# Expert weights laid out by partition, loaded in three transfers of 4 MB instead of eight of 1 or 2 MB

## The reference

```python
def moe_ffn(h, w_router, b_router, w_exp_in, b_exp_in, w_exp_out, b_exp_out):
    logits = (t @ w_router + b_router).astype(jnp.float32)
    top_val, top_idx = lax.top_k(logits, TOP_K)          # 4 of 32
    gate_w = jax.nn.softmax(top_val, axis=-1)
    ...
        hb = xb @ w_exp_in[e] + b_exp_in[e]               # 1024 x 2048
        g = jnp.minimum(hb[:, :D_FF_2], SWIGLU_LIMIT)
        u = jnp.clip(hb[:, D_FF_2:], -SWIGLU_LIMIT, SWIGLU_LIMIT)
        a = g * jax.nn.sigmoid(SWIGLU_ALPHA * g) * (u + 1.0)
        return a @ w_exp_out[e] + b_exp_out[e]            # 1024 x 1024
    ...
    y = jnp.einsum('nk,nkd->nd', gate_w, y_slot)
```

## Time and profile before

| | |
|---|---|
| median of 3 runs | 1470.51 us |
| lowest, highest | 1470.10, 1471.36 |
| span of the profiled execution, first to last instruction | 1468.7 us |
| median less that span | 1.8 us |
| mean granted PE clock | 0.984 |
| PE busy | 1308.1 us, 89% |
| DVE, ACT, POOL busy | 32%, 27%, 15% |
| HBM read | 492.76 MB, mean 336 GB/s over the span |

### The profile page before, as it was taken

One profiled execution on the slowest core, in us unless ns is written; L12 is line 12 of the kernel. 1 busy time (PEld: TensorE's weight loads), 2 busy tenths in 40 slices (PEclk: granted clock), 3 DMA queues, 4 the chain that ended last, 5 costly groups with the idle time before them and its releaser, 6 DMA issues.

```text
span 1468.7 us, 25925 instructions
## 1 busy us (share of the span) xinstructions
PE 1308.1 (89%) x9475; PEld 815.8 (56%) x9476; DVE 469.8 (32%) x916; ACT 390.4 (27%) x728; POOL 222.4 (15%) x129
## 2 busy tenths in 40 slices
PE   7998999999999997887989888988889988997886
PEld 7786999878999853343334433443333434343333
DVE  2756777654534961111102110211011101110112
ACT  5566666555667420010001000110010001000101
POOL 5772112006775300000000000000000000000000
PEclk9999999999999999898999999999999999999998
DMA  9532667855443789999999999999999999999996
GB/s 332 179 101 58 172 184 227 303 193 172 172 173 116 256 333 423 424 428 424 427 424 428 427 427 424 426 428 425 425 428 427 422 424 428 426 427 425 427 427 273
DMA packets 114537, 494.40 MB, mean 337 GB/s; under 512 B 7633, under 2 KB 57153, under 8 KB 81505
## 3 DMA queue, kind: packets, MB, share of 16 engines
q1 hardware_dynamic: 113011, 491.50, 83.3%
q10 hardware_dynamic: 1486, 2.34, 0.5%
HBM read 492.76 MB, written 1.06 MB: 336 GB/s over the span
## 4 chain that ended last, share of the span: by engine, by line
PE 59%; DMA 29%; DVE 5%; issue 4%; ACT 3%; SPq 0%; POOL 0%; DVEq 0%; ACTq 0%
DMA big_mem<-in_w_exp_in 24%; PE ps L1055 16%; PE ps L1097 8%; PE ps L579 6%; PE ps L581 5%; PE ps L580 5%; DMA big_mem<-in_w_exp_out 5%; PE ps L1038 3%; PE ps L797 1%; PE ps L799 1%; PE ps L798 1%; PE ps L1120 1%; PE ps L1111 1%; PE ps L1085 1%; PE ps L599 1%
## 5 line engine op out<-in xcount | busy, mean ns | idle before, releaser
L1055 PE MATMUL ps<-big_mem,ring_mem 128*32 128x512 f32 (+1 forms) x2304 | 366.8, 614 | 53.7 <-DMA big_mem<-in_w_exp_in 53.7
L1055 PEld LDWEIGHTS ps<-big_mem,ring_mem 128*32 128x32 f32 (+1 forms) x2304 | 111.0, 121 | 287.2 <-issue 194.4
L1097 PE MATMUL ps<-big_mem,x 128*32 128x256 f32 (+1 forms) x1888 | 185.1, 436 | 5.3 <-ACT x L1716 3.3
L579 PE MATMUL ps<-hT_hi,w_hi 128*128 128x256 f32 x600 | 171.3, 285 | 1.3 <-DVE hT_lo L1806 1.3
L580 PE MATMUL ps<-hT_lo,w_hi 128*128 128x256 f32 x600 | 169.7, 283 | 0.0
L581 PE MATMUL ps<-hT_hi,w_lo 128*128 128x256 f32 x600 | 169.7, 283 | 0.0
L1038 PEld LDWEIGHTS ps<-ring_mem,h 128*128 128x128 f32 x1024 | 131.6, 197 | 60.1 <-issue 60.1
L1038 PE MATMUL ps<-ring_mem,h 128*128 128x96 f32 x1024 | 148.9, 289 | 0.0
L2312 DVE TENSOR_SCALAR ring_mem<-ps 128x256 f32<-128x256 f32 (+1 forms) x36 | 18.7, 520 | 404.1 <-PE ps L1055 404.1
L1700 ACT ACTIVATE ring_mem<-ring_mem 128x256 f32<-128x256 f32 (+1 forms) x36 | 17.7, 493 | 466.4 <-DVE ring_mem L2312 466.4
L1097 PEld LDWEIGHTS ps<-big_mem,x 128*32 128x32 f32 (+1 forms) x1888 | 71.7, 117 | 104.9 <-issue 67.7
(11 more groups left out here) (430 smaller groups left out, 1736.6 us busy)
## 6 DMA issues: line engine op xcount, KB each, us to landing
big_mem<-in_w_exp_in SPq DMA_DIRECT2D x128, 2048.0 KB, 22.3
big_mem<-in_w_exp_out SPq DMA_DIRECT2D x128, 1024.0 KB, 21.4
ring_mem<-in_w_in SPq DMA_DIRECT2D x14, 2048.0 KB, 8.0
ring_mem<-in_w_up SPq DMA_DIRECT2D x44, 512.0 KB, 4.6
ring_mem<-in_w_down SPq DMA_DIRECT2D x5, 2048.0 KB, 11.1
ring_mem<-in_w_out SPq DMA_DIRECT2D x4, 2048.0 KB, 8.1
ring_mem<-in_w_branch_a SPq DMA_DIRECT2D x1, 2048.0 KB, 7.4
ring_mem<-in_w_branch_b SPq DMA_DIRECT2D x1, 2048.0 KB, 7.7
```

Of the source, the lines that this page charges most:

```text
L579: mm(out, hi, x_hi, start=start, stop=False)
L1055: last = mm(out, stationary, weights[:, f, w * q:w * (q + 1)] if m > XS else weights[:, :, w * q:w * (q + 1)], start=start, stop=stop)
L1097: last = mm(ps[m * q:m * (q + 1), 4 + at // XS, 0:w], aT[:, k % n, k // n, :], wout[:, k, w * q:w * (q + 1)], start=(k == 0), stop=(k == K ...
```

## The change

On the host the two weight arrays are laid out anew: matrix row 128k + p is row k of partition p, and a partition's eight rows lie end to end (64 KB of in-weights, 32 KB of out-weights). The in-weights come in two transfers of four rows k, 4 MB each with 32 KB to a partition; the out-weights in one of eight rows, 4 MB, 32 KB to a partition. PE waits for landings at k = 0 and 4 of the first product and at k = 0 of the second. SP waits for four finished rows ahead of a half of the in-weights and for all eight ahead of the out-weights. As row k now holds the matrix rows 128k to 128k + 127, the gather and the transposes of `a` read 128 columns in order instead of every second one of 256. The amount of data and the number of matmuls stay as they are.

```diff
+WIN_ROWS, WOUT_ROWS = 4, 8
...
-        win_x = ins["w_exp_in_2"].rearrange("l e (k p j) n -> (l e) k p j n", p=P, j=2)
-        wout_x = ins["w_exp_out_2"].rearrange("l e (k p j) n -> (l e) k p j n", p=P, j=2)
+        win_x = ins["w_exp_in_2"].rearrange("e p (h j) n -> e h p j n", j=WIN_ROWS)
+        wout_x = ins["w_exp_out_2"].rearrange("e p (h j) n -> e h p j n", j=WOUT_ROWS)
...
-                for k in range(KD // 2):
-                    sp.wait_ge(s["gu_part"], KD * others + 2 + 2 * k)
-                    sp.dma_start(win[:, 2 * k:2 * k + 2, :], win_x[cur, k]).then_inc(win_in[k], 16)
-                for k in range(KD // 2):
-                    sp.wait_ge(s["y_part"], KD * others + 2 + 2 * k)
-                    sp.dma_start(wout[:, 2 * k:2 * k + 2, :], wout_x[cur, k]).then_inc(wout_in[k], 16)
+                for n in range(KD // WIN_ROWS):
+                    sp.wait_ge(s["gu_part"], KD * others + WIN_ROWS * (n + 1))
+                    sp.dma_start(win[:, WIN_ROWS * n:WIN_ROWS * (n + 1), :], win_x[cur, n]).then_inc(win_in[n], 16)
+                for n in range(KD // WOUT_ROWS):
+                    sp.wait_ge(s["y_part"], KD * others + WOUT_ROWS * (n + 1))
+                    sp.dma_start(wout[:, WOUT_ROWS * n:WOUT_ROWS * (n + 1), :], wout_x[cur, n]).then_inc(wout_in[n], 16)
...
-                        last = mm(ps[:, bank, c:c + SLOTS], h1[:, t, SEQ * (k // 2) + k % 2:SEQ * (k // 2 + 1):2], moe["picks"][:, t, :], start=(t == 0), stop=(t == T - 1))
+                        last = mm(ps[:, bank, c:c + SLOTS], h1[:, t, P * k:P * (k + 1)], moe["picks"][:, t, :], start=(t == 0), stop=(t == T - 1))
...
-                    if k % 2 == 0:
-                        pe.wait_ge(win_in[k // 2], landed_all)
+                    if k % WIN_ROWS == 0:
+                        pe.wait_ge(win_in[k // WIN_ROWS], landed_all)
...
-                    last = nc.tensor.transpose(place, moe["a"][:, KD * at + SEQ * (c // 2) + c % 2:KD * at + SEQ * (c // 2 + 1):2], ident)
+                    last = nc.tensor.transpose(place, moe["a"][:, KD * at + P * c:KD * at + P * (c + 1)], ident)
...
-                    if k % 2 == 0:
-                        pe.wait_ge(wout_in[k // 2], landed_all)
+                    if k % WOUT_ROWS == 0:
+                        pe.wait_ge(wout_in[k // WOUT_ROWS], landed_all)
...
+    for n in ("w_exp_in_2", "w_exp_out_2"):
+        a = np.asarray(inputs[n])[0]
+        given[n] = np.ascontiguousarray(a.reshape(E, KD, P, a.shape[-1]).transpose(0, 2, 1, 3))
```

More of the change, by code:

```diff
@@ L129, in program @@
         s = {n: ctx.enter_context(nc.semaphore(n)) for n in EVENTS}
-        win_in = [ctx.enter_context(nc.semaphore(f"win{k}_in")) for k in range(KD // 2)]
-        wout_in = [ctx.enter_context(nc.semaphore(f"wout{k}_in")) for k in range(KD // 2)]
+        win_in = [ctx.enter_context(nc.semaphore(f"win{h}_in")) for h in range(KD // WIN_ROWS)]
+        wout_in = [ctx.enter_context(nc.semaphore(f"wout{h}_in")) for h in range(KD // WOUT_ROWS)]
         ring_mem = ctx.enter_context(nc.sbuf_tensor("ring_mem", [P, 3 * 4096], F32))
@@ L458, in _ @@
             sp.wait_ge(s["merged_ready"], KD)
-            for k in range(KD // 2):
-                sp.dma_start(win[:, 2 * k:2 * k + 2, :], win_x[0, k]).then_inc(win_in[k], 16)
+            for n in range(KD // WIN_ROWS):
+                sp.dma_start(win[:, WIN_ROWS * n:WIN_ROWS * (n + 1), :], win_x[0, n]).then_inc(win_in[n], 16)
             sp.wait_ge(s["out_ps"], T)
-            for k in range(KD // 2):
-                sp.dma_start(wout[:, 2 * k:2 * k + 2, :], wout_x[0, k]).then_inc(wout_in[k], 16)
+            for n in range(KD // WOUT_ROWS):
+                sp.dma_start(wout[:, WOUT_ROWS * n:WOUT_ROWS * (n + 1), :], wout_x[0, n]).then_inc(wout_in[n], 16)
             sp.wait_ge(s["counts_ready"], 1)
@@ L1134, in _ @@
                     c = SLOTS * (k % EARLY)
-                    last = mm(ps[:, 7 if k < EARLY else 6, c:c + SLOTS], h1[:, t, SEQ * (k // 2) + k % 2:SEQ * (k // 2 + 1):2], moe["picks"][:, t, :],
+                    last = mm(ps[:, 7 if k < EARLY else 6, c:c + SLOTS], h1[:, t, P * k:P * (k + 1)], moe["picks"][:, t, :],
                               start=(t == 0 and k in (0, EARLY)), stop=(t == T - 1), skip_group_check=True)
```

## The result

The changed kernel takes 1487.66 us (median of 4 runs), the kernel before 1470.7 on the same chip: ratio 1.0112, 95% interval 1.01 to 1.0124. It is slower, as forecast, but by 17 us where 6.3 were forecast, and 0.7 us outside the range. The profiled execution is the slowest of the four, 1489.61 with a span of 1487.8, 19.1 above the span before.

What follows compares the result with a forecast made beforehand. The weight stream through the DMA engines was taken to bound the kernel, PE a close second. Terms -9.3 + 3.5 + 9.6 + 1.1 + 1.4 = +6.3 us gave 1476.8 us, 0.4% slower; range 1465 to 1487.

Steps and rivals of the forecast that it cites:

- Pace: Weight stream: a 4 MB transfer takes 9.74 us, a turn 29.22 instead of 29.52, saving 9.3 us over 31 turns.
- Start: First load for turn 1 waits for four rows of the first product instead of two: 3.5 us more.
- Coarser release: Out-weights wait for all eight rows; the stream stands still 2.4 us in each of four 96-token turns: 9.6 us more.
- clock term: Low granted clock lengthens the first product in 96-token turns: 1.1 us more, bounds 0 and 5.4.
- first condition: PE must finish both products of a turn within four transfers, 38.96 us, from its first in-half's landing; 96 tokens need 41.35.
- In-order reads: Gather and transposes load faster on PE: 0.3 us off each 96-token turn, counted within the stall; bounds 0 to 6 us.
- End: Last second product starts all eight rows only after the whole out-weights land: 1.4 us more.
- A: Rival, faster: the stream gains more than PE's stalls give back, 4 MB in 9.60 us: 1466 us, chance 0.17.
- B: Rival, no difference: the gather gains 1 us more per 96-token turn or a transfer takes 9.68: 1472 us, chance 0.2.
- D: Rival, slower: in-weight rows 64 KB apart in memory cost 3% of their load time: 1488 us, chance 0.05.
- C: Rival, slower by more: long rows gain nothing and low clock falls into each 96-token turn: 1486 us, chance 0.15.

Runs made afterwards that it cites:

- e9: Changed kernel's transfer sizes and releases on the old weight layout (rows of 16 KB and 8 KB, strided gather and transposes): 1497.22 us, ratio 1.0181 to the kernel before.
- e1: Changed kernel with its new layout and in-order reads, but transfers of two rows as before: 1471.12 us, ratio 0.9998 to the kernel before.
- e5: Changed kernel with tokens beyond 64 of an expert left out, so 96-slot turns become 64-slot turns: 1468.04 us, ratio 0.997 to the uncapped kernel before.
- e10: Changed kernel with two more matmuls, results unused, behind the first product of each 96-slot turn: 1498.73 us, ratio 1.0179 to the kernel before.
- e11: Kernel before the change with two more matmuls, results unused, in each 96-slot turn: 1473.0 us, ratio 1.0008 to the kernel before.
- e4: Changed kernel with out-weights in two transfers of 2 MB, in-weights still in two of 4 MB: 1483.03 us, ratio 1.0081 to the kernel before.
- e2: Changed kernel with out-weights in four transfers of 1 MB, in-weights still in two of 4 MB: 1487.39 us, ratio 1.0112 to the kernel before.
- e3: Changed kernel with in-weights in four transfers of 2 MB, out-weights still in one of 4 MB: 1489.37 us, ratio 1.0118 to the kernel before.
- e8: Changed kernel with in-weights in four transfers of 2 MB and out-weights in two of 2 MB: 1468.84 us, ratio 0.9976 to the kernel before.
- e12: Changed kernel with four extra matmuls in each 32-slot turn ahead of the wait for the second in-half: 1491.2 us, ratio 1.0146 to the kernel before.
- e7: Changed kernel with ten extra matmuls in each 32-slot turn ahead of the wait for the second in-half: 1566.37 us, ratio 1.0644 to the kernel before.

## Why the prediction was right in its sign and wrong in its size

- **Pace**: right in kind, a little small. 9.3 us were forecast, 11.5 measured; a 4 MB transfer takes 9.71 and not 9.74. That the cost goes by row and not by transfer is shown by e9.
- **Start**: 3.5 forecast, 3.7 measured.
- **Coarser release**: the mechanism is the one forecast, and e1, e5, e10 and e11 show it from four sides. The size is what failed, **the term 4 x 2.4 = 9.6 with its clock term of 1.1: 10.7 us, where the stream lost 24.2, 22.5 of them around the four 96-slot turns.** Turn by turn, from landing of the first half (in the first and fourth worked out from the landing ahead, as PE did not wait there) to data flowing again, less four transfers of 9.71: 4.6, 5.3, 4.1 and 3.6 us, 17.6 in all. Of the 6.9 beyond the forecast, 5.2 are clock: the four first products took 23.47, 24.78, 23.49 and 23.04, 6.3 over 22.1, where I had counted 1.1. 0.6 is the first of the turns, which PE began late, its second product of the turn ahead having run slow behind a wait (5.02 us instead of 3.66). The rest, about 1, is what the in-order reads did not give (0.2 a turn, 0.8) and the faster transfers (four take 38.84 and not 38.96, 0.5).
- **What is left**, 24.2 - 17.6 = 6.6 us, has two parts. The landings give 22.5 around the four turns, 4.9 or some 1.2 a turn more than this reckoning, and this is not settled. The windows show that the DMA engines don't run dry together (a share of 0.08 in 948 to 949, after lower shares before it), and behind the restarts single windows are low again (229 GB/s in 810 to 811, 262 in 1172 to 1173). Two readings are open. The engines may drift apart after every common start, so that four more starts cost it four more times. Or the next in-half comes a little late for those that are ahead: SP issues it 8.9 us behind the out-weights in each of the four turns (809.87 against 800.92), and data follows an issue by 0.8. No run tells them apart.
- **A fifth loss**, 2.7 us between 649.42 and 710.40, was not in the prediction at all: its conditions were laid out for the 96-slot turns only. The row at 680.40 shows PE idle for 6.22 us ahead of a 32-slot turn, and the profile names nothing that it waits for. The kernel before has the same pause, 5.45 us ahead of 672.63, and its stream loses nothing there. In the changed kernel SP issues the next in-half only at 686.15, when by the mean pace the queue wants it at 687.6 (649.42 - 0.7 + 4 x 9.71), and from 684 to 690 us only 328 GB/s are moved. So here too a slow spell of PE that had been covered seems to reach the stream. That link is read from the trace and was not tested; e4, whose pause ends at 677.61, loses nothing between 649.10 and 707.54. This loss makes up for the about 1 us gained at start and end: 4.9 + 2.7 - 1.0 = 6.6.
- **Clock**: I took half of what two of four turns had lost before. In fact the clock was lower throughout: 0.966 over the span against 0.984 before, and below full in the windows of all four first products (0.93, 0.87, 0.93 and 0.93). The bound of 5.4 that I had written beside it was near the 6.3 measured; the value taken was the fault.
- **The second condition**, the first in-half behind the turn that follows, was missing. It doesn't change the forecast for this kernel, where the first condition hides it, but it made my expectations for e2 and e4 wrong by 18 us each.
- **In-order reads**: the loads of the transposes fell from 209 to 141 ns and those of the gather from 196 to 192, as the earlier trace rows let expect, but from first to second product of a 96-slot turn it came to 5.99 instead of 6.1 us, not 0.3 less.
- **End**: 1.4 forecast, 2.8 measured. The last turn's last four rows ran partly at 1.2 GHz, 5.34 instead of 3.64, so the second product began 2.1 us after the last byte.
- The rivals: A and B did not come about, D is refuted by e1. C had the right second half, a low clock in every 96-slot turn, and the right time (1486), but not its first half: long rows did gain.

## What to carry to other kernels

With one buffer that is refilled as it is used, the size of a transfer is also the grain in which the buffer is given back. Ask for the longest stage how long the consumer takes from the first landing to the last use that each later transfer waits for, and compare it with the transfers in between; do it for every transfer, not for the first that comes to mind. Here two conditions had slack of a few microseconds, and each of the two coarsenings alone used it up. In e2 and e3 that cost more than three times what longer rows gained (some 18 us against 5.0, some 23 against 6.8); with the grain made finer again where it mattered the kernel gained (e8).

A buffer's slack that hides a slow spell today is used up by a change that draws on it, and PE's slow spells lay in small turns too (the pause ahead of 680.40). A consumer's durations for such a sum are best taken at their worst in the trace, not at their best.

## What the runs showed of the hardware that I had not expected

A transfer's rate follows the length of its contiguous rows, even far up: 1 MB in rows of 8 KB takes 2.48 us, in rows of 16 KB 2.45 (4.90 for 2 MB), in rows of 32 KB 2.43 (9.71 for 4 MB). Four megabytes in 128 times two rows of 16 KB take 9.79 in one transfer, as in two, and 4 MB in rows of 8 KB take 9.95 in one (29.53 - 2 x 9.79 in e9), as in four (9.92).

PE's granted clock fell where its waits grew longer, even though its share of busy time stayed at 89%: 0.984 before, 0.966 with transfers of 4 MB. With four added matmuls in each 32-slot turn it was 0.982 (e12) and with ten 0.990 (e7), but there the share of busy time rose too, to 92% and 93%, so these two don't tell which of the two the clock followed.
